# VectorE adds the output tile to x before it makes the next weights' low part, at three stage ends

## The reference, cut to what matters

```
for layer in range(2):
    hn = rms_norm(x, norm_mix_g[layer])
    mix = rglru_mixer(hn, ...) if layer == 0 else dsa_mixer(hn, ...)   # both end in "... @ w_out"
    x = x + mix
    x = x + square(relu(rms_norm(x, norm_mlp_g[layer]) @ w_up)) @ w_down
x = rms_norm(x, final_norm_g); then second_block(x, ...)
```

## Time and profile before

| what | us |
|---|---|
| three timed runs | 860.76, 859.25, 860.49 |
| their median | 860.49 |
| the profiled execution | 859.15 |
| its span | 857.3 |
| TensorE (PE) busy | 851.0 |
| VectorE (DVE) busy | 652.8 |
| ScalarE (ACT) busy | 496.0 |

### The profile page before, as it was taken

The page is one execution under the profiler, slowest core; times in us unless marked ns, Lnnn a source line. Parts: engine busy times, 40 slices in busy tenths (PEclk is TensorE's granted clock), DMA queues, the critical chain, the costliest instruction groups (busy, mean ns, idle before and its releaser), DMA issues.

```text
span 857.3 us, 17572 instructions
## 1 busy us (share of the span) xinstructions
PE 851.0 (99%) x7192; PEld 832.9 (97%) x7192; DVE 652.8 (76%) x1245; ACT 496.0 (58%) x905; POOL 46.8 (5%) x63
## 2 busy tenths in 40 slices
PE   9999999999999999999999999999999999999998
PEld 8999999999999899989999999999999999999998
DVE  6978678898978688575667555566799899997873
ACT  5785787764435667577778444443546564544650
POOL 0000000000000047000000000031020000000000
DMA  9927877878978623367657855617555323565541
GB/s 301 342 66 242 256 238 259 263 267 274 311 245 277 213 99 99 99 204 238 193 178 221 242 188 197 196 51 185 165 167 183 113 75 99 164 206 191 155 147 50
DMA packets 162864, 164.22 MB, mean 192 GB/s; under 512 B 16816, under 2 KB 159328, under 8 KB 162528
## 3 DMA queue, kind: packets, MB, share of 16 engines
q1 hardware_dynamic: 161696, 162.05, 59.7%
q10 hardware_dynamic: 1088, 1.05, 0.4%
HBM read 162.01 MB, written 2.91 MB: 192 GB/s over the span
## 4 chain that ended last, share of the span: by engine, by line
PE 94%; DVE 3%; ACT 1%; DMA 1%; issue 1%; POOL 0%; ACTq 0%; DVEq 0%
PE ps L316 24%; PE ps L318 24%; PE ps L320 24%; PE ps L442 3%; PE ps L1594 2%; PE ps L1596 2%; PE ps L1592 2%; PE ps L1653 2%; PE ps L459 2%; PE ps L1688 1%; PE ps L1692 1%; PE ps L1690 1%; DVE wl L283 1%; PE ps L1634 1%; PE ps L1643 1%; PE ps L1132 1%
## 5 line engine op out<-in xcount | busy, mean ns | idle before, releaser
L283 DVE TENSOR_TENSOR wl<-raw,wh 128x1024 fp32r<-128x1024 f32 x256 | 309.2, 1224 | 27.9 <-ACT wh L276 27.7
L316 PE MATMUL ps<-xh,wh 128*128 128x256 f32 x1136 | 320.2, 282 | 1.6 <-ACT xh L390 1.6
L318 PE MATMUL ps<-xl,wh 128*128 128x256 f32 x1136 | 315.6, 278 | 0.4
L320 PE MATMUL ps<-xh,wl 128*128 128x256 f32 x1136 | 315.4, 278 | 0.0
L276 ACT ACTIVATE wh<-raw 128x1024 fp32r<-128x1024 f32 x256 | 266.9, 1051 | 69.8 <-PE ps L320 62.5
L316 PEld LDWEIGHTS ps<-xh,wh 128*128 128x128 f32 x1136 | 213.8, 188 | 4.1 <-ACT xh L390 2.0
L318 PEld LDWEIGHTS ps<-xl,wh 128*128 128x128 f32 x1136 | 214.1, 188 | 1.2 <-DVE xl L384 1.0
L320 PEld LDWEIGHTS ps<-xh,wl 128*128 128x128 f32 x1136 | 213.5, 188 | 0.0
L320 PE MATMUL ps<-hh,wl 128*128 128x256 f32 x512 | 141.3, 276 | 0.0
L316 PE MATMUL ps<-hh,wh 128*128 128x256 f32 x512 | 141.3, 276 | 0.0
L318 PE MATMUL ps<-hl,wh 128*128 128x256 f32 x512 | 141.3, 276 | 0.0
(11 more groups left out here) (358 smaller groups left out, 1415.0 us busy)
## 6 DMA issues: line engine op xcount, KB each, us to landing
raw<-in_w_in_dram SPq DMA_DIRECT2D x34, 1024.0 KB, 5.4
raw<-in_mlp_up_dram SPq DMA_DIRECT2D x32, 1024.0 KB, 5.4
raw<-in_mlp_down_dram SPq DMA_DIRECT2D x32, 1024.0 KB, 7.3
aw<-in_w_adaT_dram SPq DMA_DIRECT2D x24, 512.0 KB, 4.8
raw<-in_rec_w_in_dram SPq DMA_DIRECT2D x7, 1024.0 KB, 11.6
raw<-in_att_w_in_dram SPq DMA_DIRECT2D x6, 1024.0 KB, 6.2
raw<-in_rec_w_out_dram SPq DMA_DIRECT2D x4, 1024.0 KB, 5.9
raw<-in_att_w_o_dram SPq DMA_DIRECT2D x4, 1024.0 KB, 5.0
```

What stands on the lines that cost most here:

```text
L283: e.tensor_tensor(parts_of(i)[1], raw_of(i), f32(parts_of(i)[0]), op=ALU.subtract).then_inc(S["wl"], 1)
L316: e.matmul(o, H[:, first + n], xh[:, k], start=start and n == 0, stop=False)
L318: e.matmul(o, H[:, first + n], xl[:, k], start=False, stop=False)
L320: ins = e.matmul(o, L[:, first + n], xh[:, k], start=False, stop=stop and n == len(ks) - 1)
```

## The change

In ro and wo the call of `lows` moves from ahead of `x_add` to behind it, and so behind the wait for the product that `x_add` needs. In dn0 `vector_down`, which holds that wait, the multiplication and the addition, moves ahead of `lows` at the last piece of each output tile. The same instructions are issued, with the same operands and the same waits; their order changes on VectorE alone.

```
     def vector_ro(e, q):
         for f in range(8):
-            lows(e, q, ahead(f"ro{f}", lag(f, 7))[1])
             q.wait_ge(S["mm"], done[f"ro{f}"])
             x_add(e, q, 0, f, ps[f"ro{f}"])
+            lows(e, q, ahead(f"ro{f}", lag(f, 7))[1])
             x_low(e, q, 1, f, vc("mlp0", f))
             rms_add(e, q, 1, f)
...
                     f = 2 * j + i
+                    if k == 3:
+                        vector_down(e, q, 0, f)
                     lows(e, q, ahead(f"dn0.{f}.{k}")[1])
                     if k == 3:
-                        vector_down(e, q, 0, f)
                         x_low(e, q, 2, f, vc("mix1", f))
                         rms_add(e, q, 2, f)
...
         for f in range(8):
-            lows(e, q, ahead(f"wo{f}", lag(f, 7))[1])
             q.wait_ge(S["mm"], done[f"wo{f}"])
             x_add(e, q, 2, f, ps[f"wo{f}"])
+            lows(e, q, ahead(f"wo{f}", lag(f, 7))[1])
             x_low(e, q, 3, f, vc("mlp1", f))
             rms_add(e, q, 3, f)
```

## The result

| | before | changed |
|---|---|---|
| median of four timed runs, us | 859.87 (859.12 to 860.76) | 854.44 (853.72 to 854.61) |
| span of the profiled execution, us | 857.3 | 852.8 |

The ratio is 0.9936, with a 95% interval of 0.9921 to 0.9950. I had forecast 856.8 us and a range from 854.8: the direction is right, the mechanism in wo is the one named, but the gain is 5.4 us where the sum had 3.05.

What follows compares the result with a forecast made beforehand. PE, busy 99% of the span, was taken to bound the kernel. Gains of 2.91 us in wo, 0.14 in dn0 and 0 in ro made 3.05, so 859.87 - 3.05 = 856.8 us, range 854.8 to 860.0.

Steps and rivals of the forecast that it cites:

- the sum: Over wo, dn0 and ro: 2.91 + 0.14 + 0 = 3.05 us gained, bounds 2.6 and 3.3.
- What bounds wo, and the 2.91 us: End of wo: DVE is late, so PE waits; at 2.21 us a tile the whole 2.91 us wait goes.
- the list of what the profile would show: In wo, additions of tiles 3 to 7 follow PE's products; L333 starts 0.82 us behind the 18th matmul, not 3.73.
- The rival of no overlap: In wo, each DVE operation waits for the whole one ahead: 2.53 us a tile, 2.0 gained, 857.8 us; chance 0.05.
- dn0, 0.14 us: End of dn0: tile 7's x_low comes at 273.26 instead of 273.40, so PE gains 0.14 us.
- The upper bound of 0.42: End of dn0: most that could be gained, L318's delay of 0.31 us and about 0.1 of longer step behind it.
- The risk on the low parts: Late in dn0, low parts held behind an addition could come late; tightest margin 0.6 us, cost nothing, up to 0.3.
- ro, nothing: Behind ro: DVE adds tile 7 about 0.9 us earlier, but PE had 0.8 us to spare; worth nothing.
- the pace: Rival: PE's stretch from 383 to 418 us turns from 0.1178 to 0.1133 us a matmul; 4.2 us in all, chance 0.22.
- The likeness to the first MLP: Argument for the faster pace: PE reaches wo's sums without a wait, as behind ro, where slow turned fast at the spread.
- Its lower end, 854.8: Bottom of the range to 860.0: the faster pace's 855.7 us, with 0.9 for the scatter of the median.

Runs made afterwards that it cites:

- e2_dn0: Kernel before, with the new order in dn0 alone: 859.04 us, ratio 0.9987 to the kernel before.
- e10_before_again: Kernel before, unchanged, run again for a second profiled execution: 860.04 us.
- e6_tile7: Changed kernel, but at the very last tile of dn0 the weights' low part comes behind x_low and rms_add: 853.35 us, ratio 0.9941 to the kernel before.
- e3_ro: Kernel before, with the new order in ro alone: 859.73 us, ratio 0.9989 to the kernel before.
- e5_pace_after: Changed kernel, with two unread 128 x 128 matmuls added behind the second MLP's fourth product: 855.84 us, ratio 0.9961 to the kernel before.
- e13_half: Kernel before, with 8 unread 128 x 128 matmuls in the first of the two waits behind wo alone: 857.16 us.
- e4_pace_before: Kernel before, with two unread 128 x 128 matmuls added behind the second MLP's fourth product: 859.77 us, ratio 0.9989 to the kernel before.
- e9_fill: Kernel before, with 8 and 6 unread 128 x 128 matmuls in the two waits behind wo: 856.64 us, ratio 0.9974 to the kernel before.

## Why the prediction was wrong, step by step

- **What bounds wo, and the 2.91 us: right.** The tile costs 2.20 us against 2.21 worked out, tile 7 is added 0.03 us behind PE's last matmul, the sums follow without a wait. The one slip is in the list of what the profile would show: the additions of tiles 3 to 6 follow VectorE, and only that of tile 7 follows PE. The rival of no overlap is out, since the operations overlap as the rows had it (2.20 us for a tile, not 2.53).
- **dn0, 0.14 us: right.** L318 is 0.13 us less late, in the changed kernel and in e2_dn0. The upper bound of 0.42 was too low for what PE loses there: e6_tile7, without the late L318, is by the next product 0.45 us better than the changed kernel, and so 0.6 better than before. The risk on the low parts did not come up in the changed kernel's profile; that the margin is thin was right, but it is as thin in the kernel before (e10_before_again), so the change does not bring it.

The last operations of dn0 in the changed kernel, on VectorE; they answer to the earlier trace rows:

```profile
271.61 0.43 DVE L380 TENSOR_TENSOR x<-x,tmp 128x256 f32<-128x256 f32 x1
271.96 1.22 DVE L283 TENSOR_TENSOR wl<-raw,wh 128x1024 fp32r<-128x1024 f32 x1
273.09 0.48 DVE L384 SCALAR_TENSOR_TENSOR xl<-x,sb_vec,xh 128x256 fp32r<-128x256 f32 x1
```

And PE's matmul that waits for them, which answers to the earlier trace rows:

```profile
273.63 0.39 PE L318 MATMUL ps<-xl,wh 128*128 128x256 f32 x1
```

- **ro, nothing: right** (e3_ro).
- **The sum: wrong, by two terms.** First, the pace, which the sum put at nothing. I had it as a rival at 4.2 us and gave it 0.22, because I could not derive the phase. It came in every profile whose PE does not idle behind wo (before its pair, in e5_pace_after too) and also in e3_ro and e13_half, where PE does. The likeness to the first MLP, which I named and then did not trust, was the better guide. Between the two profiles it is worth 1.1 to 1.3 us. On average it is worth less, since the kernel before has the fast stretch in some executions: at clock 1.000 its mean is 857.6 us (16 executions) and the changed kernel's 854.2 (10), a gain of 3.4 us, give or take 0.7, where the sum without any pace had 3.05.
- Second, **the clock, which had no term at all.** I read a granted clock of 1.00 over the whole span in the one profile of before and took the wait's price to be its length. This is the step that failed most: 52 of 68 executions of the kernel before run at a lower mean clock, and none of the changed kernel's ten. Two of the five profiles in which PE idles in both waits behind wo (e4_pace_before and e10_before_again) show half the clock behind them, at a cost of 2.9 and 1.6 us. The clock costs the kernel before 2.2 us on average. The profiled execution, at 859.15 us, was one in which the clock had held, but a slow one among these (they take 855.9 to 859.7), and so it lay only 0.1 us below the fastest of the timed runs and gave no warning.
- **The size.** For the two profiles: 2.91 + 0.14 + 1.1 = 4.15, against 4.2 measured (PE's lead grows from 0.18 us to 4.4 at 416 us). For the means of all executions: 859.85 - 854.24 = 5.6 us, of which 3.4 are there at full clock and 2.2 are the clock. That the waits cause the loss of clock is shown by e9_fill and e13_half; where in the span it falls is seen in the two profiles alone.
- **The range.** Its lower end, 854.8, was the faster pace alone, less 0.9 for scatter. A range whose base is a median that scatters by 1.5 us should have asked what scatters.

What stays open: what settles the pace at the sums behind wo, and why idling of 1.9 us in all costs the clock in some executions and not in others.

## What to carry to other kernels

When one engine waits for a second one's short reply (VectorE for ScalarE's high part), put independent work into that gap, and start the step that somebody else waits for ahead of it; where the wait is the last thing in a stage, put the independent work behind everything (dn0's last tile). The price of a wait on TensorE is its length and what it does to the clock behind it, which one profile may not show: if timed runs of a kernel scatter more than its neighbour's, look at the mean granted clock of each run, and take a second profile, before pricing. Keeping TensorE busy with matmuls that nobody reads gave back about half of what removing the wait gave: 2.6 us by the means, against 5.6.

## What the runs showed of the hardware that I had not expected

- A matmul of 128 x 256 in fp32r pieces has two steps at the same full clock, 0.1133 and 0.1178 us (4% apart), kept over whole stretches: the fast one over the 128 us of the earlier trace rows, the slow one over the 35 us behind wo's spread. There they change at the small matmuls: the spread turned the pace in all 14 profiles, ten times to fast and four times to slow. The same pair of matmuls turned it in either direction (e4_pace_before, e5_pace_after) and, at another place, not at all (e14_pair585).
- Behind two waits of 1.0 and 0.9 us PE was granted 1.2 GHz instead of 2.4, for at least 6 us in one profile and 3.4 in another; 76 of 102 executions with these waits show a lower mean clock. With 14 matmuls issued into the waits, or 8 into the first alone, none of 24 does.
- VectorE started an SBUF operation 0.33 us into a 0.42 us addition that reads PSUM. The Trainium skill, page "VectorE: DVE Perf Modes", says in "The DRAIN you can't avoid" that the next operation does not start until the pipeline is empty, but that one which is not held starts earlier; this trace shows the second.
